# State-space scan in a two-block kernel: the block between the chunks computed once per group of four heads

## The chip, the cores and the metric

The kernel runs on one core of a Trainium2 chip. The metric is the device time of one execution in microseconds (us), as the median of several runs. Before the change it is 1258.52 us (three runs, 1258.48 to 1260.17). The core's engines work side by side and meet at semaphores: TensorE (PE; matmuls, with its weight loads shown apart as PEld), VectorE (DVE), ScalarE (ACT), GpSimd (POOL), and SyncE (SP), whose queue issues the weight DMAs.

## What is computed

The reference is two transformer-like blocks on 256 tokens of width 1024. Nearly all of the work is dense products with weights from HBM. The change touches one part of the second block, the state-space mixer (SSD): 32 heads of width 64 in 8 groups of four heads; the heads of a group share B and C. The 256 tokens are two chunks of 128.

```python
def step(state, inp):                      # one chunk of 128 tokens
    xc, dtc, bc, cc = inp
    cum = jnp.cumsum(dtc * A, axis=1)
    seg = cum[:, :, None] - cum[:, None, :]
    decay = jnp.exp(jnp.where(causal, seg, -jnp.inf))
    cb = jnp.einsum('btgn,bsgn->btsg', cc, bc)
    w = cb[..., None] * decay * dtc[:, None]
    y = jnp.einsum('btsgk,bsgkp->btgkp', w, xc)
    y = y + jnp.einsum('btgn,bgkpn->btgkp', cc, state) * jnp.exp(cum)[..., None]
    ...                                    # state for the next chunk
```

With two chunks and a zero first state, the output is a lower triangular 2 by 2 arrangement of 128x128 blocks per head: chunk 0 on chunk 0, chunk 1 on chunk 1 (both causal), and the block between the chunks, inputs of chunk 0 on outputs of chunk 1. A head's decay in that last block splits into a factor of the input token (decay to the end of chunk 0) and one of the output token (decay since the start of chunk 1).

## The kernel before

Weights come in "units" of up to 128x2048 float32 through a ring of five slots. ACT copies a unit to its rounded part `whi` (L830, in halves L841), DVE makes the rest `wlo` (L1310, in halves L1335), and PE does each product as three matmuls in the fast format (helper `three`, L2125 to L2127). Each engine's program is a fixed list of instructions, written out by hand and executed in order.

**The scan stage** is interleaved with the dense products of 16 units (`SSD_UNITS`): eight of the gate projection `zz`, then eight of the output projection `so`. Each unit has four steps; a step on PE is `ssd_step(n)` followed by six dense 512-column matmuls. `SSD_STEPS` says what each of the 64 steps carries. Steps 0 to 3 are empty, steps 4 to 15 are heads 0 to 11, steps 16 and 17 are empty; then head 12 (step 18), yT 0 (19), head 13 (20), yT 1 (21), heads 14 to 19 (22 to 27), two empty steps (28, 29), head 20 (30), yT 2 (31), head 21 (32), yT 3 (33), heads 22 to 27 (34 to 39), two empty (40, 41), head 28 (42), yT 4 (43), head 29 (44), yT 5 (45), heads 30 and 31 (46, 47), and the tail (48). ACT, DVE and PE each walk this list in their own order:

- SP broadcasts the head's decay row from DRAM to a ring of six buffers `dec` (L680), POOL adds a causal mask to the two diagonal blocks (L787).
- ACT, `decay(h)` (L1110): two exponentials over 256 and 128 columns, after POOL's mask. Between them it does the halves of `whi`, the tanh of the gates (L1123, in units 2, 4, 6, 8), the copies `xs_copy` (L854), the norm scaling (L1108) and the transposed output (L864).
- DVE, at head h: multiplies the 384 decay columns with the group's scores in PSUM bank `CB` (L1933). At h%8==6 it adds the y bank of the even group (L1879), at h%8==7 `prepare` makes the next eight heads' inputs (L1869 and L1873, four instructions of 512 columns), at h%8==2 it adds the odd group and gates (L1888), at h%8==3 `group_stats` (L1901). Further there are halves of `wlo` (two per four steps), the gate product (L1923) at the third step of units 2, 4, 6, 8, and at yT steps the low part (L1364).
- PE, at head h's step: `ssd_y_of(h - 2)`, three matmuls of 128x64 (L2729 to L2731), each in two passes. The step before a new group also computes that group's scores (`ssd_scores`, L2716 and L2717). At a yT step it transposes finished output (L2748).

So the product of head h is two head steps behind its place in the DVE list. Ahead of the stage, around line 1830 and 2688, the cumulative sums of all heads are made, negated, transposed and stored as rows of 384 columns.

Of the kernel before, what the change touches and what calls it, by code (L numbers as in the profile page):

```python
# [33 lines left out]
F32 = mybir.dt.float32  # L34
# [448 lines left out]
def build(nc, w, out):  # L483
# [3 lines left out]
    with ctx:  # L487
# [31 lines left out]
        crow = sb("crow", [SSD_HEADS, TRI])  # L519
        dec0 = sb("dec0", [P, TRI])  # L520
        decay_rows = nc.dram_tensor("decay_rows", (SSD_HEADS, TRI), F32, kind="Internal").ap()
# [55 lines left out]
        dec = [dec0[:, :]] + [rows[:, 1, TRI * b:TRI * b + TRI] for b in range(2)] + [room(14336 + TRI * b, TRI) for b in range(3)]  # L577
# [43 lines left out]
        dt_sum, dt_log, dta_ready, cum_row = sem("dt_sum"), sem("dt_log"), sem("dta_ready"), sem("cum_row")  # L621
# [45 lines left out]
        def _(sp):  # L667
# [46 lines left out]
        def _(pool):  # L714
# [66 lines left out]
            pool.wait_ge(cum_row, 1)  # L781
            pool.dma_start(decay_rows[:, :], crow[:, :]).then_inc(rows_stored, 16)
            for h in range(SSD_HEADS):
                pool.wait_ge(row_landed[h % SSD_RING], 16 * (h // SSD_RING + 1))
                d = dec[h % SSD_RING]
                diagonal = d.rearrange("p (a t) -> p a t", a=3)[:, 0:3:2, :]
# [26 lines left out]
        def _(act):  # L813
# [287 lines left out]
            nc.scalar.preload_act_table_set("exp_and_others")  # L1101

# [7 lines left out]
            def decay(h):  # L1110
                act.wait_ge(row_masked, h + 1)
                d = dec[h % SSD_RING]
                A(d[:, 0:T], d[:, 0:T], ACT.Exp, bias=negcum[:, 0, 0, h:h + 1])
                A(d[:, T:TRI], d[:, T:TRI], ACT.Exp, bias=negcum[:, 1, 0, h:h + 1]).then_inc(s_exp, 1)

            for u in range(SSD_UNITS):
                for n, (what, h) in enumerate(SSD_STEPS[SSD_PER_UNIT * u:SSD_PER_UNIT * (u + 1)]):
# [12 lines left out]
                    if what == "head":  # L1130
                        if h > 0:
                            decay(h)
# [158 lines left out]
        def _(dve):  # L1291
# [529 lines left out]
            for m in range(16):  # L1821
# [4 lines left out]
                if m == 5:  # L1826
# [3 lines left out]
                    V.tensor_scalar(negcum[:, :, :, :], sums.unsqueeze(2).to_broadcast([P, NT, 2, SSD_HEADS]), -1.0, None, ALU.mult)\  # L1830
                        .then_inc(done("cum"), 1)
                if m == 7:
                    b = wait_bank(dve, "cumT")
                    H = SSD_HEADS
                    mark(V.tensor_scalar(crow[:, 0:P], b[0:H, 0:P], -1.0, None, ALU.mult))
                    V.tensor_scalar(crow[:, 2 * P:TRI], b[0:H, P:2 * P], -1.0, None, ALU.mult).then_inc(done("cumT"), 1)
                    dve.wait_ge(dve_step, steps[0])
                    wait_drained(dve, "cumT")
                    V.tensor_scalar(crow[:, P:2 * P], crow[:, 2 * P:TRI], crow[:, P - 1:P], None, ALU.add).then_inc(cum_row, 1)
# [11 lines left out]
                if m == 0:  # L1851

                    dve.wait_ge(dt_log, 2)
# [5 lines left out]
            def prepare(q):  # L1859
# [11 lines left out]
                for t in range(NT):  # L1871
                    x3 = xsN[:, t, cols].rearrange("p (h d) -> p h d", d=SSD_P)
                    V.tensor_tensor(x3, x3, dtv[:, t, hs].unsqueeze(2).to_broadcast([P, 8, SSD_P]), ALU.mult).then_inc(xdt_ready, 1)  # L1873

# [33 lines left out]
            prepare(0)  # L1908
            last_norm = [what for what, _ in SSD_STEPS].index("tail") // SSD_PER_UNIT
            for u in range(SSD_UNITS):  # L1910
                for n, (what, h) in enumerate(SSD_STEPS[SSD_PER_UNIT * u:SSD_PER_UNIT * (u + 1)]):
# [13 lines left out]
                    if what == "head":  # L1925
# [3 lines left out]
                        if h > 8 and h % 8 == 3:  # L1929
# [179 lines left out]
        def _(pe):  # L2109
# [569 lines left out]
            for m, j in enumerate(BC_ORDER):  # L2679
                if m >= 2:  # L2680
                    b_unit(at[("bc", j)], h_hi, h_lo, one(("bc", j)), ready=(lambda k: second_block() if k == 3 else None) if m == 2 else None)
                if m == 4:

                    pe.wait_ge(dta_ready, 2)
                    pe.wait_ge(cst_in, 16)
                    b = claim("cum")
                    for t in range(NT):
                        last = M(b[:, SSD_HEADS * t:SSD_HEADS * (t + 1)], tri, dta[:, t, :], start=True, stop=True)
                    last.then_inc(fill("cum"), 1)
                if m == 7:  # L2690
                    wait_drained(pe, "cum")
                    b = claim("cumT")
                    for t in range(NT):
                        last = nc.tensor.transpose(b[0:2 * SSD_HEADS, P * t:P * t + P], negcum[:, t, :, :].rearrange("p a h -> p (a h)"), ident)
# [16 lines left out]
            y_bank, so_banks = [], []  # L2711

            def ssd_scores(g):
# [3 lines left out]
                M(b[:, T:TRI], bcT[:, g, P:T], bcT[:, 8 + g, P:T], start=True, stop=True).then_inc(fill(("CB", g)), 1)  # L2717

            def ssd_y_of(h):
# [5 lines left out]
                if h % 4 == 0:  # L2725
                    y_bank[:] = [claim(("y", h // 4))]
                y_0, y_1 = [y_bank[0][:, T * t + SSD_P * (h % 4):T * t + SSD_P * (h % 4) + SSD_P] for t in range(NT)]
                s = dec[h % SSD_RING]
                M(y_0, s[:, 0:P], xsN[:, 0, xs], start=True, stop=True)  # L2729
                M(y_1, s[:, P:T], xsN[:, 0, xs], start=True, stop=False)  # L2730
                M(y_1, s[:, T:TRI], xsN[:, 1, xs], start=False, stop=True).then_inc(ssd_y, 1)  # L2731

            def ssd_step(n):
                what, h = SSD_STEPS[n]
                if what == "head":
                    if h >= 2:
                        ssd_y_of(h - 2)
                if what == "tail":
# [246 lines left out]
```

## Time and profile before

| | |
|---|---|
| median of 3 runs | 1258.52 us |
| span of the profiled execution | 1257.2 us |
| PE busy | 1242.1 us (99%) |
| DVE busy | 932.5 us (74%) |
| ACT busy | 684.2 us (54%) |
| POOL busy | 68.2 us (5%) |
| DMA queue with the weights | 53.5% of 16 engines' span |
| scan stage | about 671 to 779 us |

The span is the profiled time from first to last instruction; the time of a run lies 1.3 us above it. "Busy" counts instructions, and a PE row's length includes its pipeline's drain, so the distance between two starts is what a matmul costs in a stream. A bracket behind a row is the engine's idle time before it, with what ended it.

### The profile page before, as it was taken

The numbers are of one execution on the slowest core, as the hardware profiler recorded it, in microseconds if no ns is written. First come the engines' busy times: TensorE is split into PE (matmuls) and PEld (weight loads), VectorE is DVE, ScalarE is ACT, GpSimd is POOL, SyncE is SP. The second block draws the span as 40 slices with busy tenths as digits, with TensorE's granted clock in tenths as the row PEclk, the third lists the DMA queues.
The fourth block names the chain that finished last, engine by engine and source line by source line (L and its number), as shares of the span: only waits on it lengthen the run. The fifth ranks groups of instructions, "written<-read, shape, count | busy, mean of one in ns | idle before, by whom it ended". The sixth has DMA issues, their size and how long they took to land. (4 is left out here: it accounts for less than half of the span.)

```text
span 1257.2 us, 18334 instructions
## 1 busy us (share of the span) xinstructions
PE 1242.1 (99%) x7514; PEld 1102.9 (88%) x7514; DVE 932.5 (74%) x1292; ACT 684.2 (54%) x872; POOL 68.2 (5%) x93
## 2 busy tenths in 40 slices
PE   9999999999999999999999999999999999999997
PEld 8878999989988888889998888888888888888886
DVE  6676857875456666577997998788888868788877
ACT  6654444343553444455777655466655574566652
POOL 2000000100000000000003331000000000000000
PEclk9999999999999999999999999999999999999999
DMA  9664545656435665647656654655554744655551
GB/s 294 219 184 144 185 143 188 214 186 209 168 101 170 199 194 178 197 138 219 185 168 210 203 191 151 217 185 201 184 186 138 231 134 134 201 194 179 197 194 41
DMA packets 162595, 227.97 MB, mean 181 GB/s; under 512 B 7853, under 2 KB 123825, under 8 KB 162384
## 3 DMA queue, kind: packets, MB, share of 16 engines
q1 hardware_dynamic: 159392, 216.68, 53.5%
q0 software_dynamic: 2816, 9.52, 2.3%
q8 instruction: 60, 0.98, 0.3%
q10 hardware_dynamic: 304, 0.59, 0.1%
q14 instruction: 23, 0.19, 0.0%
HBM read 225.68 MB, written 1.10 MB: 180 GB/s over the span
## 5 line engine op out<-in xcount | busy, mean ns | idle before, releaser
L1310 DVE TENSOR_TENSOR wlo<-raw,whi 128x2048 fp32r<-128x2048 f32 (+3 forms) x185 | 415.9, 2260 | 113.9 <-ACT whi L830 112.8
L830 ACT ACTIVATE whi<-raw 128x2048 fp32r<-128x2048 f32 (+3 forms) x185 | 345.9, 1883 | 16.0 <-DMA raw<-in_w_xkv 6.1
L2159 PE MATMUL psum<-h_both,whi 128*128 128x512 f32 x714 | 254.7, 396 | 0.0
L2158 PE MATMUL psum<-h_both,wlo 128*128 128x256 f32 x714 | 199.4, 279 | 0.3 <-DVE h_both L1364 0.3
L2125 PE MATMUL psum<-h_both,whi 128*128 128x256 f32 x688 | 195.9, 285 | 0.0
L2127 PE MATMUL psum<-h_both,wlo 128*128 128x256 f32 x688 | 194.6, 283 | 0.0
L2126 PE MATMUL psum<-h_both,whi 128*128 128x256 f32 x688 | 194.6, 283 | 0.0
L2125 PE MATMUL psum<-whi,r_hi 128*128 128x512 f32 x446 | 176.6, 396 | 0.0
L2127 PE MATMUL psum<-whi,r_lo 128*128 128x512 f32 x446 | 173.9, 390 | 0.0
L2126 PE MATMUL psum<-wlo,r_hi 128*128 128x512 f32 x446 | 173.8, 390 | 0.0
L2159 PEld LDWEIGHTS psum<-h_both,whi 128*128 128x128 f32 x714 | 134.0, 188 | 27.6
L2158 PEld LDWEIGHTS psum<-h_both,wlo 128*128 128x128 f32 x714 | 134.6, 189 | 5.2 <-DVE h_both L1364 0.6
L2125 PEld LDWEIGHTS psum<-h_both,whi 128*128 128x128 f32 x688 | 131.9, 192 | 0.4 <-issue 0.3
L2126 PEld LDWEIGHTS psum<-h_both,whi 128*128 128x128 f32 x688 | 131.9, 192 | 0.2
L2127 PEld LDWEIGHTS psum<-h_both,wlo 128*128 128x128 f32 x688 | 131.9, 192 | 0.0
L2125 PE MATMUL psum<-whi,h_both 128*128 128x512 f32 (+4 forms) x304 | 118.7, 391 | 0.4 <-issue 0.3
L1964 DVE SCALAR_TENSOR_TENSOR arena<-arena,pv 128x256 f32<-128x256 f32 x176 | 77.3, 482 | 51.7 <-ACT arena L1165 43.9
L2127 PE MATMUL psum<-whi,h_both 128*128 128x512 f32 (+4 forms) x304 | 113.5, 373 | 0.0
L2126 PE MATMUL psum<-wlo,h_both 128*128 128x512 f32 (+4 forms) x304 | 113.1, 372 | 0.0
L2127 PEld LDWEIGHTS psum<-whi,r_lo 128*128 128x128 f32 x446 | 83.7, 188 | 17.9
L2126 PEld LDWEIGHTS psum<-wlo,r_hi 128*128 128x128 f32 x446 | 83.9, 188 | 16.5
L2125 PEld LDWEIGHTS psum<-whi,r_hi 128*128 128x128 f32 x446 | 83.8, 188 | 15.3
(350 smaller groups left out, 1807.1 us busy)
## 6 DMA issues: line engine op xcount, KB each, us to landing
raw<-in_ffn_up SPq DMA_DIRECT2D x40, 1024.0 KB, 5.1
raw<-in_w_in SPq DMA_DIRECT2D x31, 1024.0 KB, 5.8
raw<-in_ssd_in_proj SPq DMA_DIRECT2D x22, 1024.0 KB, 5.4
raw<-in_ffn_down SPq DMA_DIRECT2D x22, 1024.0 KB, 4.9
raw<-in_w_up SPq DMA_DIRECT2D x16, 1024.0 KB, 5.6
raw<-in_w_down SPq DMA_DIRECT2D x16, 1024.0 KB, 4.9
raw<-in_w_xkv SPq DMA_DIRECT2D x8, 1024.0 KB, 5.2
raw<-in_ssd_out_proj SPq DMA_DIRECT2D x8, 1024.0 KB, 5.2
```

Source lines behind the costliest of these rows:

```text
L830: A(whi[u % SLOTS][:, 0:kt * n], raw[u % SLOTS][:, 0:kt * n], ACT.Copy).then_inc(hi_split, 1)
L1310: V.tensor_tensor(wlo[s][:, 0:kt * n], raw[s][:, 0:kt * n], whi[s][:, 0:kt * n].bitcast(F32), ALU.subtract).then_inc(lo_split, 1)
L1964: ins = V.scalar_tensor_tensor(y, fpad[g % 2][x][:, ct, tap:tap + T], pv[:, wcol:wcol + 1], y, ALU.mult, ALU.add)
L2125: M(o, a_hi, b_hi, start=start, stop=False)
L2126: M(o, a_hi, b_lo, start=False, stop=False)
L2127: return M(o, a_lo, b_hi, start=False, stop=stop_)
L2158: M(b[:, 0:T], w_lo_k, h_hi[:, k, :], start=False, stop=False)
L2159: return M(b[:, :], w_hi_k, h_both[:, :, k, :], start=False, stop=k == kt - 1)
```

## The change

The block between the chunks is no longer part of each head's matrix. `dec` has 256 columns per head, the two diagonal blocks; the decay rows are 256 long. Per group of four heads there is one product instead: PE takes the copied scores block `cbT` as stationary and the group's inputs scaled to the end of chunk 0 (`x_end`, 256 columns) as moving operand, DVE scales the result in PSUM in place, and the heads' own products accumulate on top. The order of the lists (`SSD_STEPS`) is the same.

```diff
+        after = dec0[:, 0:P]
+        x_end = [dec0[:, 0:T], room(14848, T)]
+        cbT = [room(15104 + P * b, P) for b in range(2)]
+        to_end, since = negcum[:, 0, 1, :], negcum[:, 1, 1, :]
...
-                elif h == 3:
+                elif h == 4:
                     wait_bank(sp, ("xsN", 7))
...
-            rows_at = {at[("zz", 0, 0)] + SLOTS - 1: [0, 1, 2], at[("zz", 0, 1)] + SLOTS: [3, 4, 5]}
+            rows_at = {at[("zz", 0, 0)] + SLOTS - 1: [0, 1, 2, 3], at[("zz", 0, 1)] + SLOTS: [4, 5]}
...
             nc.scalar.preload_act_table_set("exp_and_others")
+            wait_drained(act, "cum")
+            A(to_end, to_end, ACT.Exp).then_inc(factors_ready, 1)
+            A(since, negcum[:, 1, 0, :], ACT.Exp, scale=-1.0).then_inc(factors_ready, 1)
+
+            def copy_scores(g):
+                b = wait_bank(act, ("CB", g))
+                if g >= 2:
+                    act.wait_ge(off_done, g - 1)
+                A(cbT[g % 2], b[:, P:T], ACT.Copy).then_inc(cb_copied, 1)
...
-                A(d[:, 0:T], d[:, 0:T], ACT.Exp, bias=negcum[:, 0, 0, h:h + 1])
-                A(d[:, T:TRI], d[:, T:TRI], ACT.Exp, bias=negcum[:, 1, 0, h:h + 1]).then_inc(s_exp, 1)
+                A(d[:, 0:P], d[:, 0:P], ACT.Exp, bias=negcum[:, 0, 0, h:h + 1])
+                A(d[:, P:T], d[:, P:T], ACT.Exp, bias=negcum[:, 1, 0, h:h + 1]).then_inc(s_exp, 1)
...
                     if what == "head":
+                        if h % 4 == 0:
+                            copy_scores(h // 4)
                         if h > 0:
                             decay(h)
...
+            def scale_to_end(g):
+                dve.wait_ge(xdt_ready, 2 * (g // 2) + 2)
+                dve.wait_ge(factors_ready, 2)
...
+                V.tensor_tensor(x_end[g % 2].rearrange("p (h d) -> p h d", d=SSD_P),
+                                xsN[:, 0, 256 * g:256 * g + 256].rearrange("p (h d) -> p h d", d=SSD_P),
+                                to_end[:, heads].unsqueeze(2).to_broadcast([P, 4, SSD_P]), ALU.mult).then_inc(x_end_ready, 1)
+
+            def scale_off(g):
+                dve.wait_ge(off_done, g + 1)
+                y = bank[use[("y", g)][0]][:, T:2 * T].rearrange("p (h d) -> p h d", d=SSD_P)
+                V.tensor_tensor(y, y, since[:, 4 * g:4 * g + 4].unsqueeze(2).to_broadcast([P, 4, SSD_P]), ALU.mult).then_inc(off_scaled, 1)
...
             prepare(0)
+            scale_to_end(0)
...
                         b = wait_bank(dve, ("CB", h // 4))
-                        V.tensor_tensor(dec[h % SSD_RING], dec[h % SSD_RING], b[:, 0:TRI], ALU.mult)\
+                        if h % 4 == 0:
+                            dve.wait_ge(cb_copied, h // 4 + 1)
+                        d = dec[h % SSD_RING].rearrange("p (a t) -> p a t", a=2)
+                        V.tensor_tensor(d, d, b[:, 0:2 * T].rearrange("p (a t) -> p a t", a=2)[:, :, 0:P], ALU.mult)\
                             .then_inc(done(("CB", h // 4)) if h % 4 == 3 else s_w, 1)
+                        if h % 4 == 1:
+                            scale_off(h // 4)
                         if h % 8 == 6:
                             add_sums(2 * q)
                         if h % 8 == 7 and q < 3:
                             prepare(q + 1)
+                        if h % 4 == 3 and h < SSD_HEADS - 1:
+                            scale_to_end(h // 4 + 1)
...
+                    last = M(b[:, 2 * SSD_HEADS:3 * SSD_HEADS], after, dta[:, 0, :], start=True, stop=True)
...
+            def ssd_off(g):
+                pe.wait_ge(cb_copied, g + 1)
+                pe.wait_ge(x_end_ready, g + 1)
+                y_next[:] = [claim(("y", g))]
+                M(y_next[0][:, T:2 * T], cbT[g % 2], x_end[g % 2], start=True, stop=True).then_inc(off_done, 1)
...
                 if h % 4 == 0:
-                    y_bank[:] = [claim(("y", h // 4))]
+                    y_bank[:] = y_next
+                    pe.wait_ge(off_scaled, h // 4 + 1)
...
-                M(y_0, s[:, 0:P], xsN[:, 0, xs], start=True, stop=True)
-                M(y_1, s[:, P:T], xsN[:, 0, xs], start=True, stop=False)
-                M(y_1, s[:, T:TRI], xsN[:, 1, xs], start=False, stop=True).then_inc(ssd_y, 1)
+                M(y_0, s[:, 0:P], xsN[:, 0, xs], start=False, stop=True, skip_group_check=True)
+                M(y_1, s[:, P:T], xsN[:, 1, xs], start=False, stop=True, skip_group_check=True).then_inc(ssd_y, 1)
...
                     if h >= 2:
                         ssd_y_of(h - 2)
+                    if h % 4 == 0:
+                        ssd_off(h // 4)
```

Ahead of the stage, `crow` is made by one DVE instruction instead of three, the copy of `to_end` and the mask `after` are one small DVE instruction each, and the two transposes of the sums have 32 columns instead of 64.

## Rows read from the trace of the kernel before

**Rows 1.** The page: busy time by engine, and the granted clock in 40 slices

```profile
PE 1242.1 (99%) x7514; PEld 1102.9 (88%) x7514; DVE 932.5 (74%) x1292; ACT 684.2 (54%) x872; POOL 68.2 (5%) x93
...
PEclk9999999999999999999999999999999999999999
```

**Rows 2.** Waits of PE, 600 to 800 us: us in total, times, longest us

```profile
PE psum L2748 <- ACT arena L1108: 0.9, 3, 0.3
```

**Rows 3.** Timeline of PE, steps 34 to 36: start, length, engine, line, shapes

```profile
735.30 0.33 PE L2729 MATMUL psum<-arena,rows 128*128 128x64 f32 x2
735.47 0.39 PE L2730 MATMUL psum<-arena,rows 128*128 128x64 f32 x2
735.69 0.39 PE L2731 MATMUL psum<-arena,rows 128*128 128x64 f32 x2
735.89 0.48 PE L2125 MATMUL psum<-whi,r_hi 128*128 128x512 f32 x1
...
737.36 0.33 PE L2729 MATMUL psum<-arena 128*128 128x64 f32 x2
...
737.97 0.65 PE L2716 MATMUL psum<-arena 128*128 128x256 f32 x2
738.46 0.38 PE L2717 MATMUL psum<-arena 128*128 128x128 f32 x2
...
740.08 0.33 PE L2729 MATMUL psum<-arena 128*128 128x64 f32 x2
```

**Rows 4.** Timeline of PE, start of step 4, then head 1's product at step 7

```profile
673.37 0.47 PE L2125 MATMUL psum<-whi,h_both 128*128 128x512 f32 x1
...
678.94 0.43 PE L2729 MATMUL psum<-arena,rows 128*128 128x64 f32 x2 [0.30 <-DVE rows L1933]
```

**Rows 5.** Timeline of ACT at the start of the stage

```profile
672.19 1.28 ACT L1101 ACT_TABLE_LOAD   x1
673.48 1.06 ACT L841 ACTIVATE whi<-raw 128x1024 fp32r<-128x1024 f32 x1
674.45 0.49 ACT L1113 ACTIVATE dec<-dec,negcum 128x256 f32<-128x256 f32 x1
...
675.14 1.05 ACT L841 ACTIVATE whi<-raw 128x1024 fp32r<-128x1024 f32 x1
676.09 0.57 ACT L854 ACTIVATE arena<-psum 128x512 f32<-128x512 f32 x1
676.56 1.05 ACT L841 ACTIVATE whi<-raw 128x1024 fp32r<-128x1024 f32 x1
```

**Rows 6.** Timeline of PE, the product of head 2 at step 8

```profile
681.75 0.33 PE L2729 MATMUL psum<-arena,rows 128*128 128x64 f32 x2
```

**Rows 7.** Timeline of DVE, steps 33 to 36

```profile
735.05 0.88 DVE L1364 SCALAR_TENSOR_TENSOR r_lo<-psum,pv,r_hi 128x256 fp32r<-128x256 f32 x2 [1.32 <-ACT r_hi L864]
...
737.04 0.55 DVE L1933 TENSOR_TENSOR arena<-arena,psum 128x384 f32<-128x384 f32 x1
737.50 0.68 DVE L1879 TENSOR_TENSOR arena<-arena,psum 128x512 f32<-128x512 f32 x1
...
739.24 0.54 DVE L1933 TENSOR_TENSOR arena<-arena,psum 128x384 f32<-128x384 f32 x1
...
743.03 0.54 DVE L1933 TENSOR_TENSOR dec<-dec,psum 128x384 f32<-128x384 f32 x1
```

**Rows 8.** Timeline of PE, transposes of yT 1 and yT 3

```profile
708.75 0.60 PE L2748 MATMUL psum<-cst,arena 128*128 128x128 f32 x4
...
733.47 0.60 PE L2748 MATMUL psum<-cst,arena 128*128 128x128 f32 x4
```

**Rows 9.** Timeline of DVE around the other two `prepare`

```profile
685.11 0.56 DVE L1933 TENSOR_TENSOR arena<-arena,psum 128x384 f32<-128x384 f32 x1 [0.31 <-ACT arena L1114]
...
693.50 0.54 DVE L1933 TENSOR_TENSOR rows<-rows,psum 128x384 f32<-128x384 f32 x1
...
716.81 0.54 DVE L1933 TENSOR_TENSOR arena<-arena,psum 128x384 f32<-128x384 f32 x1
```

More of the change, by code:

```diff
@@ L518, in build @@
         expa = sb("expa", [P, SSD_HEADS])
-        crow = sb("crow", [SSD_HEADS, TRI])
+        crow = sb("crow", [SSD_HEADS, T])
         dec0 = sb("dec0", [P, TRI])
-        decay_rows = nc.dram_tensor("decay_rows", (SSD_HEADS, TRI), F32, kind="Internal").ap()
+        decay_rows = nc.dram_tensor("decay_rows", (SSD_HEADS, T), F32, kind="Internal").ap()
         ARENA = 15500
@@ L576, in build @@
         yN = [room(12288 + 1024 * b, NT, MIX) for b in range(2)]
-        dec = [dec0[:, :]] + [rows[:, 1, TRI * b:TRI * b + TRI] for b in range(2)] + [room(14336 + TRI * b, TRI) for b in range(3)]
+        dec = [rows[:, 1, T * b:T * b + T] for b in range(4)] + [room(14336 + T * b, T) for b in range(2)]
+        after = dec0[:, 0:P]
+        x_end = [dec0[:, 0:T], room(14848, T)]
+        cbT = [room(15104 + P * b, P) for b in range(2)]
+        to_end, since = negcum[:, 0, 1, :], negcum[:, 1, 1, :]
         knT, vmN, qnT = room(0, 8, T), room(2048, NT, D), room(4096, 8, T)
@@ L620, in build @@
         low_out = sem("low_out")
-        dt_sum, dt_log, dta_ready, cum_row = sem("dt_sum"), sem("dt_log"), sem("dta_ready"), sem("cum_row")
+        dt_sum, dt_log, dta_ready = sem("dt_sum"), sem("dt_log"), sem("dta_ready")
+        factors_ready, cb_copied, x_end_ready, off_done, off_scaled = (
+            sem(n) for n in ("factors_ready", "cb_copied", "x_end_ready", "off_done", "off_scaled"))
         s_conv, s_silu, xdt_ready, s_w, ssd_y, y_done = (sem(n) for n in ("s_conv", "s_silu", "xdt_ready", "s_w", "ssd_y", "y_done"))
@@ L1829, in _ @@
                     sums = b[:, 0:2 * SSD_HEADS].rearrange("p (t h) -> p t h", t=NT)
-                    V.tensor_scalar(negcum[:, :, :, :], sums.unsqueeze(2).to_broadcast([P, NT, 2, SSD_HEADS]), -1.0, None, ALU.mult)\
-                        .then_inc(done("cum"), 1)
+                    V.tensor_copy(to_end, b[:, 2 * SSD_HEADS:3 * SSD_HEADS])
+                    V.tensor_scalar(negcum[:, :, 0, :], sums, -1.0, None, ALU.mult).then_inc(done("cum"), 1)
                 if m == 7:
                     b = wait_bank(dve, "cumT")
[L1834 to L1839, printed above, removed]
+                    V.tensor_scalar(crow[:, :], b[0:SSD_HEADS, 0:T], -1.0, None, ALU.mult).then_inc(done("cumT"), 1)
                 wait_drained(dve, key)
@@ L1851, in _ @@
                 if m == 0:
+                    V.tensor_scalar(after, tri, -1.0, 1.0, ALU.mult, ALU.add).then_inc(dta_ready, 1)
                     dve.wait_ge(dt_log, 2)
@@ L1873, in prepare @@
                     V.tensor_tensor(x3, x3, dtv[:, t, hs].unsqueeze(2).to_broadcast([P, 8, SSD_P]), ALU.mult).then_inc(xdt_ready, 1)
+            def scale_to_end(g):
+                dve.wait_ge(xdt_ready, 2 * (g // 2) + 2)
+                dve.wait_ge(factors_ready, 2)
+                if g == 1:
+                    wait_bank(dve, ("xsN", 7))
+                if g >= 2:
+                    dve.wait_ge(off_done, g - 1)
+                heads = slice(4 * g, 4 * g + 4)
+                V.tensor_tensor(x_end[g % 2].rearrange("p (h d) -> p h d", d=SSD_P),
[5 more added lines that the diff above has]
+                V.tensor_tensor(y, y, since[:, 4 * g:4 * g + 4].unsqueeze(2).to_broadcast([P, 4, SSD_P]), ALU.mult).then_inc(off_scaled, 1)
             def add_sums(g):
@@ L2682, in _ @@
                 if m == 4:
-                    pe.wait_ge(dta_ready, 2)
+                    pe.wait_ge(dta_ready, 3)
                     pe.wait_ge(cst_in, 16)
@@ L2687, in _ @@
                     for t in range(NT):
-                        last = M(b[:, SSD_HEADS * t:SSD_HEADS * (t + 1)], tri, dta[:, t, :], start=True, stop=True)
+                        M(b[:, SSD_HEADS * t:SSD_HEADS * (t + 1)], tri, dta[:, t, :], start=True, stop=True)
+                    last = M(b[:, 2 * SSD_HEADS:3 * SSD_HEADS], after, dta[:, 0, :], start=True, stop=True)
                     last.then_inc(fill("cum"), 1)
@@ L2693, in _ @@
                     for t in range(NT):
-                        last = nc.tensor.transpose(b[0:2 * SSD_HEADS, P * t:P * t + P], negcum[:, t, :, :].rearrange("p a h -> p (a h)"), ident)
+                        last = nc.tensor.transpose(b[0:SSD_HEADS, P * t:P * t + P], negcum[:, t, 0, :], ident)
                     last.then_inc(fill("cumT"), 1)
@@ L2708, in _ @@
             xs_transpose(6)
-            y_bank, so_banks = [], []
+            y_bank, y_next, so_banks = [], [], []
             def ssd_scores(g):
```

4 lines of the change are left out of this document (2 added, 2 removed).

## The prediction

> **What bounds the kernel now.** I read the page first [rows 1]: PE is busy for 1242.1 of 1257.2 us, and every slice shows the granted clock at 9, the higher of its two levels, 2.4 GHz. So the kernel ends when PE's list ends, and a change counts by what it does to that list: the work in it, and the gaps at its waits. Work saved on DVE or ACT is worth nothing unless PE waits for it. Second, the waits of PE around the scan stage [rows 2]: 0.9 us at three of the transposes, whose input comes from ACT. Third, the timelines of PE, ACT and DVE in the stage, side by side. They say how far each engine is from PE's next need, and that decides here, because the change adds waits to PE.
>
> **PE's work.** The three matmuls of a head start at 735.30, 735.47 and 735.69, the dense product after them at 735.89 [rows 3]. A middle one takes 0.22 us, and the whole block 0.59. Taking one out of each of 32 heads saves 32 x 0.22 = 7.0 us (6.3 at the mean of 0.20). The Trainium skill has a rule that would price this otherwise ("TensorE: Matmul & The Clock Gate", section "Back-to-back issue gap"): start to start is the column count over 2.4 GHz plus 2.5 ns, so two passes of 64 columns cost 0.06 us and the 32 removed ones 1.8 us. The rows show 0.11 us per pass, which is that page's time for a weight load of 128 columns (section "LDWEIGHTS"); with such a load before each pass, the measured 0.22 us is the price to take.
>
> Added are eight products of 128x256. The nearest row has the same shape: the scores' first product starts at 737.97 and its successor at 738.46 [rows 3], so 0.49 us, eight times 3.9 us. The product at step 4 stands alone between dense ones; after such a block the first dense matmul is late by some 0.1 us. The third column block in `cum` ahead of the stage is at most one small matmul, 0.2 us. Sum: -7.0 + 3.9 + 0.1 + 0.2 = **-2.8 us**, between -2.0 and -3.2.
>
> For the waits I need the length of PE's steps. A step with a head takes 2.06 us now (735.30 to 737.36), and the step with scores 2.72 us (737.36 to 740.08) [rows 3]. An empty step is 2.06 - 0.59 - 0.08 = 1.39 us. After the change a head's block takes 0.37 to 0.39, so its step takes 1.84 us, with scores 2.5.
>
> **The wait at step 4.** `ssd_off(0)` waits for `copy_scores(0)`. PE begins step 4 at 673.37 [rows 4]. In ACT's list the copy comes after the table load, half a unit, `decay(0)`, the other half and `xs_copy(7)`; ACT gets there at 676.56 [rows 5]. Added before it are the two exponentials of 128x32. No row of the stage has that size; two exponentials over 384 columns take 0.69 us (674.45 to 675.14), so a small one takes between 0.1 and 0.3, and I take 0.3 for both, with 0.2 and 0.6 as ends. `decay(0)` is 0.1 shorter. The copy of 128 columns ends 0.3 to 0.4 after its start (the 512-column one takes 0.57). It is done at 676.56 + 0.3 - 0.1 + 0.35 = 677.1, so PE stands still for **3.8 us** (3.6 to 4.1). Queued behind PE's waiting instruction are all dense products. `decay(1)` and the half units sit behind the copy on ACT, later by 0.5 us only, which the pause of PE covers. What goes in return: from step 4 to head 2's product at step 8 PE takes 8.38 us (673.37 to 681.75) [rows 4, 6], where the steps' work is 1.37 + 1.45 + 2.06 + 2.71 = 7.6. So 0.8 us of waiting for ACT and DVE is there already, the 0.30 at 678.94 among it [rows 4], and the new pause swallows it.
>
> **The wait at the even groups.** `ssd_off(g)` also waits for `x_end`. In DVE's list `scale_to_end(g)` stands behind head 4g-1; where g is even it thereby stands behind the whole `prepare` too. Before, the first thing PE needed from behind `prepare` was head 4g's matrix, two head steps later. Now it needs it at head 4g's own step.
>
> DVE doesn't run ahead of PE there, since it is tied to it shortly before: at yT steps its L1364 waits for ACT's copy of PE's transpose (idle 1.32 us) [rows 7]. So the times can be counted from PE's transpose, whatever was delayed earlier.
> - New DVE prices: 384 columns last 0.55 us and 512 columns 0.68 [rows 7], that is 0.13 per 128 columns. `dec` times scores becomes 0.13 shorter. `scale_to_end` and `scale_off`, 256 columns, last 0.42; overlapped with their neighbours they add 0.33 each (384 columns add 0.46, from 737.04 to 737.50).
> - Group 6: PE's yT 3 is at 733.47 [rows 8], DVE is through `prepare` at 743.03 [rows 7], 9.56 later. Two shorter products and the new scaling make it 9.56 - 0.26 + 0.33 = 9.6. PE arrives after 1.81 (transposes, six dense ones) + 1.84 + 2.5 + 0.39 = 6.5. Pause: **3.1 us**.
> - Group 4: yT 1 at 708.75 [rows 8], `prepare` over at 716.81 [rows 9], so 8.06, then 8.1 against 6.5: **1.6 us**. It is shorter because no gate product (L1923) falls between.
> - Group 2: here DVE hangs on ACT, whose tanh needs the banks full at PE's step 8; head 5 waits 0.31 for it at 685.11, and `prepare` is over at 693.50 [rows 9], 11.75 after PE's step 8 at 681.75 [rows 6]. With `scale_off(1)`, `scale_to_end(2)`, three shorter products and a shorter `decay`: 11.9. PE arrives after 2.3 + 1.84 + 1.84 + 2.5 + 0.39 = 8.9. Pause: **3.0 us**, or 2.3 if this `prepare` is as quick as the next.
>
> Between them each estimate can be off by 0.5 us.
>
> **Waits that stay covered.** At odd groups there is no `prepare` before the scaling and, from group 3, two empty steps; the margin is smallest at group 5, which has a gate product in between. `off_scaled` is needed at head 4g+2's step and stands behind head 4g+1 on DVE. After a pause PE takes 0.49 + 1.45 + 1.84 = 3.8 us to get there, DVE 0.33 + 1.14 + 0.33 + 0.33 = 2.1 (a half unit is the 1.14, from 737.50 + 0.60 to 739.24 [rows 7]). At group 1 there is no pause before: DVE's head 5 is 3.36 us after PE's step 8 (685.11 less 681.75) [rows 6, 9], the scaled result 0.33 - 0.1 + 0.33 later, at 3.9; PE gets there after 2.3 + 1.84 = 4.1, a margin of 0.2 us. Claiming the y bank two steps earlier waits for nothing: the bank's last sum is in DVE's list before the `x_end` that PE waits for anyway. ACT's copies of groups 1 to 7 have a dense block of 1.4 us to hide in, and ACT is waiting at that time. The three waits for the transposes, 0.9 us [rows 2], go away, since DVE starts its chain to them from the end of PE's pause. POOL's masks and SP's decay rows keep their places, and the rows are shorter; both follow PE's pace, as SP's weights do.
>
> **Sum.** 3.8 + 3.0 + 1.6 + 3.1 = 11.5 us of pauses, -0.8 and -0.9 for waits that they replace, -2.8 of work: +7.0. Span 1257.2 + 7.0 = 1264.2. The run's time stands 1.3 us above the span, so **1265.5 us**. Nothing behind the stage gives it back: PE has no gap there that these pauses could fill. With the low and high end of each term the sum runs from +4 to +9.5: 1262.5 to 1268.
>
> **Rivals.**
> - *The clock falls.* No row of before shows PE below the higher level, but none shows a pause of 3 us either. The Trainium skill (same page, section "HAM oscillation — how this bites in real kernels") says that a long pause between bursts of matmuls sends the clock back to the low level until PE has been busy again. At half the clock a step's six dense matmuls take 1.4 us more. Two or three such steps behind one pause: 2.8 to 4.2 us, about 1269 us. The pauses at step 4 and group 6 are the candidates. For it: their length. Against: they are single pauses in dense work. 12%.
> - *Only the pause at step 4 is real*, because DVE is earlier at the even groups than I count. It would have to gain 3 us on PE between the transpose and `prepare`, but its list there is full. Then +3.8 - 1.7 - 2.8 = -0.7: 1257.8 us, no difference. 9%.
> - *All is hidden* and PE's lighter list decides: -2.8 - 1.7 gives 1254 us. The point from which this holds is an ACT that reaches the copy by 673.4 as well, and it is 3 us late by its own rows [rows 5]. 4%.
> - *The scaled result is late too.* If the margins of 0.2 and 0.7 us at groups 1 and 5 are gone, 1 to 2 us are added: 1267 us. 5%, inside the range.
> - The forecast: 70%.
>
> **Range and chances.** 1260.5 to 1269.5 us takes in the forecast's own range, the late scaling and half of the clock's case, and leaves out the two hidden cases. A measurement of this kernel tells 0.2% (2.5 us) from no change. Faster by more: 5%; within: 10%; slower by more: 85%.
>
> **What would show it.** In the waits of PE after: one of 3.5 to 4 us released by ACT at step 4, and three released by DVE's scaling before the products of groups 2, 4 and 6, of 3.0, 1.6 and 3.1 us. PE's busy time lower by 3 us. The clock at 9 in all slices, else the first rival holds. No wait left at the transposes. If the pause at group 6 is under 1.5 us, DVE was less tied to PE than its rows say, and the middle of the sum is wrong. If a head's block falls by less than 0.15 us, the price of the removed matmul was wrong.

## The result and the profile after

The changed kernel takes 1274.0 us (median of 4 runs, 1273.33 to 1275.31) against 1259.35 us for the kernel before in the same comparison: ratio 1.0119, 95% interval 1.0107 to 1.0131. It is slower, as forecast, but by 14.7 us, where 7.0 was forecast and the range ended at 1269.5 us.

The page of the changed kernel, the lines that answer to [rows 1]:

```profile
span 1271.5 us, 18290 instructions
...
PE 1245.3 (98%) x7468; PEld 1104.9 (87%) x7468; DVE 933.4 (73%) x1308; ACT 682.4 (54%) x882; POOL 69.1 (5%) x93
...
PEclk9999999999999999999999899999999999999999
```

PE has 46 instructions fewer and is busy 3.2 us longer, and one slice of the clock shows 8. PE's waits between 600 and 800 us, the answer to [rows 2] (total, times, longest):

```profile
PE psum L2765 <- issue: 8.7, 3, 3.2
PE psum L2765 <- ACT arena L1116: 3.8, 1, 3.8
```

L2765 is the shared product. The wait for ACT's copy is the one at step 4; the other three, which the view puts down to "issue", end when DVE's scaling to the chunk's end is done. The waits at the transposes are gone. PE's timeline at the four places where it paused (start, length, bracket: idle time before):

```profile
677.41 0.67 PE L2765 MATMUL psum<-dec,arena 128*128 128x256 f32 x2 [3.83 <-ACT arena L1116]
677.73 0.58 PE L2165 MATMUL psum<-whi,h_both 128*128 128x512 f32 x1
678.15 0.40 PE L2166 MATMUL psum<-wlo,h_both 128*128 128x512 f32 x1
678.38 0.40 PE L2167 MATMUL psum<-whi,h_both 128*128 128x512 f32 x1
...
679.35 0.63 PE L2167 MATMUL psum<-whi,h_both 128*128 128x512 f32 x1
679.78 0.63 PE L2165 MATMUL psum<-whi,h_both 128*128 128x512 f32 x1
...
698.55 0.67 PE L2765 MATMUL psum<-dec,arena 128*128 128x256 f32 x2 [2.99 <-issue]
...
726.06 0.72 PE L2765 MATMUL psum<-dec,arena 128*128 128x256 f32 x2 [2.53 <-issue]
...
754.26 1.19 PE L2765 MATMUL psum<-dec,arena 128*128 128x256 f32 x2 [3.18 <-issue]
```

The pauses are 3.83, 2.99, 2.53 and 3.18 us. Behind the first one, dense matmuls start 0.23 us apart at 678.15 and 0.43 apart at 679.35: PE has gone to half its clock. The same in a table by stretch (PE, PEld, DVE, ACT, POOL busy, then the granted clock, DMA share, GB/s):

```profile
668.00:700.00 32.00, 25.17 (x121) 21.05 (x120) 24.06 (x38) 20.41 (x45) 9.03 (x10) 0.93 0.51 166
700.00:730.00 30.00, 27.47 (x133) 23.25 (x133) 24.40 (x46) 17.27 (x37) 8.96 (x10) 0.90 0.47 142
730.00:766.00 36.00, 32.82 (x165) 27.73 (x165) 29.54 (x60) 15.94 (x37) 10.87 (x11) 0.95 0.46 139
```

Before, the clock is 1.00 in all of them. Microsecond by microsecond behind the first pause it reads:

```profile
678.00:679.00 1.00, 1.00 (x6) 0.75 (x5) 1.00 (x2) 1.00 (x4) 0.19 (x1) 0.88 0.36 125
679.00:680.00 1.00, 1.00 (x4) 0.81 (x3) 1.00 (x4) 1.00 (x3) 1.00 (x2) 0.50 0.00 0
680.00:681.00 1.00, 1.00 (x3) 0.77 (x3) 1.00 (x1) 0.97 (x3) 0.29 (x1) 0.50 0.00 0
681.00:682.00 1.00, 1.00 (x4) 0.74 (x3) 1.00 (x3) 0.00 (x0) 0.00 (x0) 0.50 0.00 0
682.00:683.00 1.00, 1.00 (x8) 0.92 (x7) 0.04 (x1) 0.00 (x0) 0.00 (x0) 0.92 0.00 0
```

The shares of the clock that are missing in these five rows (0.12, 0.5, 0.5, 0.5 and 0.08 us) make 1.7 us. That is what one low stretch costs if PE works all through it. Over 671 to 801 us the mean clock is 0.95, so all four cost about 130 x 0.05 = 6.5 us.

The account of the span: +12.5 us of pauses, +6.5 of low clock, -1.7 for waits that are gone, -2.8 for PE's lighter list: +14.5. Measured: 1271.5 - 1257.2 = 14.3. The pauses and the clock are read from this trace; -1.7 and -2.8 are the forecast's own terms. PE's busy time bears the last one out: it grew by 3.2 us although 6.5 us of low clock are in it, so the work itself is some 3.3 us less.

### The profile page after: what moved, and what is told of

It reads as the page before. It is cut to its first block, busy times and chain, and to the rows that moved or that the text cites. A ratio compares the mean times of both kernels' runs of the same rounds, so it can differ in the third digit from the quotient of the medians.

```text
span 1271.5 us, 18290 instructions
## 1 busy us (share of the span) xinstructions
PE 1245.3 (98%) x7468; PEld 1104.9 (87%) x7468; DVE 933.4 (73%) x1308; ACT 682.4 (54%) x882; POOL 69.1 (5%) x93
## 4 chain that ended last, share of the span: by engine, by line
PE 90%; DVE 5%; issue 2%; ACT 2%; DMA 1%; SPq 0%; DVEq 0%
PE psum L2165 20%; PE psum L2167 20%; PE psum L2166 20%; PE psum L2199 13%; PE psum L2198 7%; PE psum L2196 2%; PE psum L2197 1%; DVE xn L1498 1%; DVE xn L1488 1%; DVE psum L1474 1%; DVE bn L1475 1%; PE psum L2779 1%; PE psum L2545 1%; PE psum L2524 1%; DMA raw<-in_w_in 1%
## 5 line engine op out<-in xcount | busy, mean ns | idle before, releaser
L2165 PE MATMUL psum<-whi,h_both 128*128 128x512 f32 (+4 forms) x304 | 120.9, 398 | 0.8 <-issue 0.7
L2167 PE MATMUL psum<-whi,h_both 128*128 128x512 f32 (+4 forms) x304 | 115.1, 378 | 0.0
```

The source lines that it names most:

```text
L2165: M(o, a_hi, b_hi, start=start, stop=False)
L2167: return M(o, a_lo, b_hi, start=False, stop=stop_)
```

## The experiments

Medians stand beside the kernel before in the same comparison, whose median lay between 1258.77 and 1258.94 us.

One thing outside the stage blurs differences of 1 to 2 us. Near 980 us PE waits twice for a norm on DVE. Here are these waits (total, times, longest) and the 15 us around them, first in the kernel before and then in a8_stats_first, a variant described below:

```profile
PE psum L2239 <- DVE xn L1481: 1.5, 2, 0.9
975.00:990.00 15.00, 13.44 (x82) 12.51 (x81) 12.90 (x22) 6.48 (x8) 2.22 (x4) 1.00 0.79 206
```

```profile
PE psum L2242 <- DVE xn L1481: 1.5, 2, 0.9
975.00:990.00 15.00, 13.44 (x72) 12.67 (x71) 11.51 (x20) 6.17 (x8) 2.13 (x4) 0.89 0.73 199
```

The waits are the same, but only the second execution has a low stretch behind them, worth 15 x 0.11 = 1.7 us. The traces of a4, a7 and f1 have it too, and each of these is one of its kernel's longer executions; those of a1, f2 and f3 don't, and are among the shorter ones. So a median can move by up to 1.6 us with how many of its executions have this stretch.

**Theory A:** each long pause of PE brings a low stretch, and these are what the forecast's sum lacked. **Rival B:** the low clock comes from the narrow products or from DVE's added work. Two kernels take pauses away.

```diff
 a2_no_rescale
-                        if h % 4 == 3 and h < SSD_HEADS - 1:
-                            scale_to_end(h // 4 + 1)
+                        if h == 3:
+                            scale_to_end(1)
...
-                pe.wait_ge(x_end_ready, g + 1)
+                pe.wait_ge(x_end_ready, min(g, 1) + 1)
```

> The changed kernel with the scaling to the chunk's end made for groups 0 and 1 only; the later groups' shared products use these two again, so nothing stands behind prepare for PE (the shared block's numbers are those of other groups). Theory A (each long pause of PE is followed by a stretch at the low clock, which costs 1.6 us more): the pauses of 3.0, 2.5 and 3.2 us go with three low stretches, 13.4 us below the changed kernel: 1260.6 us, one low stretch left, near step 4. Rival B (the low clock comes from the narrow products or from the added DVE work, not from the pauses): four low stretches stay, 8.7 us below: 1265.3 us.

1263.69 us, ratio 1.0034 (1.0022 to 1.0046). The three pauses are gone, and so are three of the four low stretches; in the stage the clock is below 1.00 only from 678 to 682 us. The narrow products are all still there, so they don't lower it; of DVE's added work a part is left out here, and a5_off_later below settles that half of B. But the time is 3 us above what A alone gives. PE's waits show most of it:

```profile
PE psum L2765 <- ACT arena L1116: 3.8, 1, 3.8
PE psum L2778 <- DVE psum L1905: 2.7, 3, 1.1
```

L1905 is `scale_off`. With the pauses at the even groups out of the way, the scaled result is late for heads 8, 16 and 24: the forecast's fourth rival, which the pauses had hidden. The profiled execution took 1262.2 us; the median, 1.5 us higher, belongs to executions with a lower mean clock (0.995 or 0.996 where it has 0.997).

```diff
 a3_copy_first
-        cbT = [room(15104 + P * b, P) for b in range(2)]
+        cbT = [dec0[:, T:TRI], room(15232, P)]
...
+            copy_scores(0)
             for u in range(SSD_UNITS):
...
-                        if h % 4 == 0:
+                        if h > 0 and h % 4 == 0:
                             copy_scores(h // 4)
```

> The changed kernel with ACT's copy of group 0's scores moved from behind xs_copy(7) to right behind the two small exponentials (its buffer moved to a free place). PE's pause at step 4 should shrink from 3.8 to 0.8 us. Theory A: with its low stretch gone, 4.6 us below the changed kernel, up to 0.8 us of it back as the old waits at heads 0 and 1: 1269.4 to 1270.2 us. Rival B (the low clock is not due to the pause): 3.0 us below or less: 1271 us or more, and the granted clock near 679 us still low.

1272.73 us, ratio 1.0107 (1.0091 to 1.0122). A miss by 3 us. The copy is early, but now PE waits 1.58 us for DVE's `x_end` at step 4 and 1.41 us for the scaled result at head 0. The pause was split rather than removed, so 0.8 us of it and one low stretch of 1.7 us are gone. That gives 1271.5 us, which two of the four executions show (1271.2 and 1271.9 us, mean clock 0.995). The other two (1273.6 and 1274.4 us, 0.992), of which the profiled one is the first, have more low clock: the low stretch with the pause of group 6 is twice as long, and one comes near 996 us, behind the waits for the norm.

```profile
748.00:760.00 12.00, 8.90 (x36) 7.35 (x35) 9.34 (x16) 4.07 (x9) 1.68 (x3) 0.72 0.39 118
990.00:1002.00 12.00, 10.09 (x51) 9.32 (x50) 9.47 (x15) 3.25 (x5) 1.64 (x3) 0.86 0.63 170
```

What A says holds: behind the two short pauses no row shows a lowered clock before 694 us.

a4_both has both of these edits.

> Both edits: copy first, and no rescaling behind prepare (the later groups' shared products use group 0's and 1's inputs). No pause above 1 us is left. Theory A: no low stretch; the changed kernel less 13.4 and 4.2: 1256.4 us, below the kernel before, ratio 0.998; up to 1.3 us more if the waits at the transposes return. Rival B: low stretches remain: 1262 us or more.

1260.4 us, ratio 1.0010 (1.0001 to 1.0020). No pause is above 1.5 us and the clock is 1.00 throughout the stage, as A has it. The missing 4 us are again DVE's:

```profile
PE psum L2779 <- DVE psum L1906: 4.3, 4, 1.4
PE psum L2766 <- DVE dec L1898: 1.3, 1, 1.3
```

**The step moved, the work kept.** 

```diff
 a5_off_later (PE)
-                    if h % 4 == 0:
+                    if h % 4 == 1:
                         ssd_off(h // 4)
```

> The changed kernel with the shared product of each group issued one head step later on PE (at head 4g+1 instead of 4g). PE comes 1.5 to 1.9 us later to each wait: pauses of about 2.3, 1.1, 0.7 and 1.3 us instead of 3.8, 3.0, 2.5 and 3.2, together 7.1 us less. Theory A (the low stretch needs a long pause): at most one low stretch is left, 4.8 us less again: 1262 us. If even the short pauses are followed by a low stretch: 1267 us. If the scaled result is then late for head 4g, 1 to 2 us come on top at each group.

1263.92 us, ratio 1.0042 (1.0027 to 1.0058). One move by one step takes away 10 of the 14.7 us, with all of the change's work kept. The pauses are 2.40, 1.17, 0.58 and 1.22 us, and only the first has a low stretch (granted clock in the last but two column):

```profile
677.00:682.00 5.00, 4.82 (x16) 4.03 (x17) 4.60 (x8) 3.78 (x9) 1.52 (x2) 0.66 0.24 85
696.00:701.00 5.00, 3.89 (x18) 3.07 (x19) 4.88 (x9) 1.01 (x3) 0.73 (x1) 1.00 0.61 224
```

The narrow products and DVE's added work are all there, and three low stretches are gone with the long pauses. So B is out.

**Pauses by themselves**, in the kernel before, in a part that the change doesn't touch:

```diff
 c1_pauses
             for what, g in MLP_ORDER[2:-2]:
+                if (what, g) in PAUSES:
+                    pe.wait_ge(idled, sum(PAUSE_OPS[:PAUSES.index((what, g)) + 1]))
...
+            for i, (what, g) in enumerate(PAUSES):
+                pool.wait_ge(unit_used, at[("down", g - 2)] + 1)
+                for j in range(PAUSE_OPS[i]):
+                    ins = nc.gpsimd.tensor_tensor(idle2[:, :, :], big2, big2, ALU.add).then_inc(idled, 1)
+                    pool.wait_ge(idled, sum(PAUSE_OPS[:i]) + j + 1)
```

> The kernel before with eleven pauses of PE in the first block's MLP, far from the scan: at the start of units up 3 to up 13 PE waits for 1, 2, 3, 4, 5, 1, 2, 3, 4, 5 and 3 instructions of POOL, each about 0.8 us, started when PE's last unit is done. The pauses should be about 1, 1.8, 2.6, 3.4, 4.2 us and so on, 28 us in all. Theory A: behind the pauses of 2.5 us and more the granted clock falls for some 3 us (cost 1.6 us each, six or seven times, 10 us), behind the short ones it stays: 1298 us. If a low stretch follows only some of them, the pause's place counts too. If it never falls here, a pause alone isn't enough, and the cause in the scan stage is something else: 1288 us.

1339.2 us (one run). The pauses came out longer than planned, 2.1 to 6.9 us and 56.4 in all, since POOL's first instruction of each pause lasted 1.9 to 2.3 us and the second 2.5, where only the further ones took 0.6. The total is 80.4 us over the kernel before, so 24 us more than the pauses. Three places of 8 us, with pauses of 2.44, 5.45 and 2.14 us:

```profile
418.00:426.00 8.00, 5.56 (x24) 4.60 (x23) 4.78 (x2) 1.63 (x1) 2.29 (x1) 0.79 0.43 136
454.00:462.00 8.00, 5.55 (x18) 4.74 (x19) 1.24 (x1) 0.00 (x0) 2.32 (x2) 0.57 0.21 74
511.00:519.00 8.00, 5.86 (x34) 5.10 (x34) 4.27 (x2) 1.12 (x1) 1.94 (x1) 1.00 0.44 131
```

The clock fell with the first two and stayed at 1.00 with the third. So a pause alone is enough, with neither narrow products nor DVE's work in play. Ten of eleven pauses, all but that of 2.14 us, have low clock with them. From each pause's end on it adds up to 46 us, in which PE works at half its speed: 23 of the 24 us, or some 2.3 us for each of the ten. The planned short pauses weren't reached here; the other kernels supply them.

**Why group 4's pause was longer than forecast.** 

```diff
 a6_no_masks
-                nc.gpsimd.tensor_tensor(diagonal, diagonal, big2, ALU.add).then_inc(row_masked, 1)
+                nc.gpsimd.tensor_tensor(d[:, 0:1], d[:, 0:1], big2[:, 0, 0:1], ALU.add).then_inc(row_masked, 1)
...
-                A(d[:, 0:P], d[:, 0:P], ACT.Exp, bias=negcum[:, 0, 0, h:h + 1])
+                A(d[:, 0:P], d[:, 0:P], ACT.Exp, scale=0.0)
```

> The changed kernel with POOL's mask cut to one column, and the exponentials taken of zero (the decays are then all one). It asks why prepare took 4.35, 3.94 and 3.6 us at groups 2, 4 and 6 where its four instructions take 2.6 us at the start of the stage. Theory: POOL's masks of 128x256 run beside it and slow DVE; then prepare takes 2.6 us everywhere, the pauses shrink to about 1.3, 1.2 and 2.2 us, and the time falls by 4 us and by up to three low stretches of 1.6 us: 1265 to 1270 us. Rival (the slow instructions are slow by themselves or through ACT): no change of prepare, 1274 us.

1264.35 us (one run). `prepare` of group 2, first in the changed kernel, then without the masks (DVE's timeline):

```profile
693.68 2.05 DVE L1882 TENSOR_TENSOR arena<-arena,row_d 128x512 f32<-128x512 f32 x2
695.76 2.23 DVE L1886 TENSOR_TENSOR arena<-arena,dtv 128x512 f32<-128x512 f32 x2
698.03 0.42 DVE L1897 TENSOR_TENSOR dec<-arena,negcum 128x256 f32<-128x256 f32 x1
```

```profile
692.77 1.29 DVE L1882 TENSOR_TENSOR arena<-arena,row_d 128x512 f32<-128x512 f32 x2
694.10 1.29 DVE L1886 TENSOR_TENSOR arena<-arena,dtv 128x512 f32<-128x512 f32 x2
695.43 0.42 DVE L1897 TENSOR_TENSOR dec<-arena,negcum 128x256 f32<-128x256 f32 x1
```

4.35 us become 2.66, so POOL's masks beside it cost DVE up to 1.7 us. The product with PSUM (L1969) lasts 0.41 us in both kernels: of the two kinds, those with two inputs from SBUF are slowed. ACT isn't the cause, although a6_no_masks changes its exponentials too: at the start of the changed kernel's stage `prepare` has ACT busy beside it, but no mask, and its instructions take 0.69 us each. This agrees with the Trainium skill, "SBUF — State Buffer", section "SBUF: two separate sides", which has DVE instructions with two SBUF inputs compete with POOL for a shared port.

**What PE's lighter list is worth.** The forecast counted -2.8 us in full.

```diff
 a1_no_between
-                M(y_1, s[:, P:T], xsN[:, 0, xs], start=True, stop=False)
-                M(y_1, s[:, T:TRI], xsN[:, 1, xs], start=False, stop=True).then_inc(ssd_y, 1)
+                M(y_1, s[:, T:TRI], xsN[:, 1, xs], start=True, stop=True).then_inc(ssd_y, 1)
```

> The kernel before with the middle matmul of each head left out (32 products of 128x64; the block between the chunks is then missing from the output). It measures PE's removed work by itself. Forecast's price, 0.22 us each: 7.0 us below the kernel before, ratio 0.9944. Rival, a pass priced by its columns alone (0.06 us each): 1.8 us below, ratio 0.9985. A third possibility: part of it comes back as longer waits for DVE at heads 0 and 1 and at the transposes, then 5 to 6 us.

1256.9 us, ratio 0.9984 (0.9975 to 0.9994): only 2.0 us. By the time alone the rival price (1.8 us) would seem to fit, but the profile says otherwise: the span is 2.4 us shorter, PE is busy 5.9 us less, and its waits are longer than in [rows 2]:

```profile
PE psum L2747 <- ACT arena L1108: 4.0, 3, 1.8
PE psum L2729 <- DVE rows L1933: 1.1, 2, 0.6
```

The waits for ACT grew by 3.1 us and those for DVE by 0.8, and 2.4 + 3.9 = 6.3 us, or 0.20 for each matmul. So the price of a removed matmul was about right (0.22, with 0.20 as its mean), but what came late next was the chain to the transposes: sums, gate, statistics (DVE), root (POOL), scaling (ACT). **Theory C:** this chain sets the pace as soon as PE is quicker. **Rival D:** DVE is full everywhere, so moving one piece only makes another late. The test takes a half unit of 1.2 us out of the chain:

```diff
 a7_lighter_stats_first (on a1), a8_stats_first (on before), f2_mended (on f1)
+                    behind = what == "head" and h > 8 and h % 8 == 3
-                    if n == 3 and u < last_norm:
+                    if n == 3 and u < last_norm and not behind:
                         lo_half(0)
...
                             .then_inc(done(("CB", h // 4)) if h % 4 == 3 else s_w, 1)
+                        if behind:
+                            lo_half(0)
```

> As a1_no_between (the middle matmul of each head left out, so the block between the chunks is missing), and DVE's half unit of 1.2 us at heads 11, 19 and 27 moved from ahead of group_stats to behind the head's product. In a1_no_between only 2.0 of 7.0 us arrived, and PE waited 0.97, 1.77 and 1.28 us at the transposes of yT 0, 2 and 4. Theory C (the chain sums, gate, statistics on DVE, root on POOL, scaling on ACT sets the pace of the stage, not PE's list): the chain is 1.14 us shorter, so these waits fall to 0, 0.6 and 0.15 us: 3.2 us less than a1_no_between, 1253.7 us, ratio 0.9960. Rival D (the waits are only the visible part of a DVE that is full everywhere): DVE is late at another place instead, 1256 to 1257 us.

1254.17 us, ratio 0.9965 (0.9953 to 0.9977): 2.7 us less than a1_no_between. PE's waits for ACT at the transposes are 1.0 us instead of 4.0. C holds; D has a small part, since one wait of 0.8 us for DVE is new.

> The kernel before with only the move of the half unit behind group_stats, nothing left out. Its waits at the transposes cost some 0.4 us each over three places. Theory C: they vanish, 1.0 to 1.3 us less, ratio 0.9991. Rival D: no difference.

1257.96 us, ratio 0.9991 (0.9982 to 1.0000). The waits at the transposes are gone from the profile. The interval touches 1, so the gain of about 1 us is likely rather than certain.

**Mended versions.** f1_mended keeps all the work of the change:

```diff
 f1_mended (besides copy_scores(0) as in a3 and ssd_off as in a5)
-                    if n == 1 and 0 < u < last_norm:
+                    if n == 1 and 0 < u < last_norm and not late(what, h):
                         lo_half(1)
...
                         if h % 8 == 7 and q < 3:
-                            prepare(q + 1)
+                            prepare(q + 1, (0,))
                         if h % 4 == 3 and h < SSD_HEADS - 1:
                             scale_to_end(h // 4 + 1)
+                        if h > 0 and h % 8 == 0:
+                            prepare(q, (1,))
...
-                        if h % 4 == 1:
+                        if h % 4 == 1 and h > 1 or h == 0:
                             scale_off(h // 4)
+                        if n == 1 and 0 < u < last_norm and late(what, h):
+                            lo_half(1)
```

Here `late` is true at head 8q+1 from q = 1 on.

> The changed kernel mended: ACT copies group 0's scores right behind the small exponentials; PE's shared product comes at head 4g+1; DVE makes the first token tile of prepare and then the scaling to the chunk's end, the second tile after the next head's product, and the half unit at the step of head 8q+1 after the scaled result. No work is left out. By the rows: PE reaches the shared product of groups 4 and 6 about 8.4 us after its transpose, DVE has the scaled inputs after 6.7 and 7.9, so no pause there. Theory A: no low stretch, PE's lighter list counts: 2.5 to 4 us below the kernel before, 1256 us, ratio 0.9975. Rival (DVE is full, and each moved piece makes something else late): small waits of 0.5 to 1.5 us at heads 8, 16, 24 and at the transposes, 1259 to 1263 us.

1259.76 us, ratio 1.0005 (0.9996 to 1.0013): in the stage no pause is above 1.33 us and no low stretch is left. It is 14 us better than the change, and no different from the kernel before. The rival was right. What is left:

```profile
PE psum L2807 <- ACT arena L1123: 2.6, 3, 1.3
PE psum L2787 <- DVE psum L1906: 0.8, 2, 0.5
```

> f1_mended with the half unit moved behind group_stats. f1_mended waited 0.85, 1.33 and 0.38 us at the transposes. Theory C: 2.4 us less than f1_mended, 1257.4 us, ratio 0.9987 to the kernel before. Rival D (DVE is full): the scaled results or heads' products are late instead, 1259 us, ratio 1.000.

1258.02 us, ratio 0.9990 (0.9981 to 0.9999): 1.7 us less. As C says, the wait of 2.6 us falls, to 0.2. The medians understate it. By time and mean clock only three of f2's eleven executions are of the shorter kind, without the low stretch near 980 us (1256.3 to 1256.8 us, clock 0.999; the others 1257.9 to 1258.6 us, 0.997 or 0.998). The five shortest of f1 lie at 1258.6 to 1259.1 us. Shorter against shorter, the move is worth 2.2 us.

```diff
 f3_pool (on f2: DVE's scaling to the chunk's end, from the second group on, goes to POOL)
-                        if h % 4 == 3 and h < SSD_HEADS - 1:
-                            scale_to_end(h // 4 + 1)
...
             for h in range(SSD_HEADS):
+                if h % 4 == 1 and h > 1:
+                    g = h // 4
+                    pool.wait_ge(xdt_ready, 2 * (g // 2) + 1)
...
+                    pool.wait_ge(off_done, max(g - 1, 1))
+                    nc.gpsimd.tensor_tensor(x_end[g % 2].rearrange("p (h d) -> p h d", d=SSD_P),
...
```

> f2_mended with the scaling to the chunk's end of groups 1 to 7 made by POOL, ahead of its mask for head 4g+1, instead of DVE. DVE's list is 7 x 0.33 = 2.3 us shorter. If DVE's fullness is what is left: 0.5 to 1.5 us less than f2_mended, 1256.5 us. Rival: POOL's instruction runs beside DVE's and slows it as the masks do, or POOL delays the masks and with them ACT's decays: 0 to 2 us more than f2_mended.

1255.83 us, ratio 0.9976 (0.9966 to 0.9986). This beats both kernels: 3.1 us below the kernel before, 18 below the change. PE's waits:

```profile
PE psum L2798 <- DVE psum L1916: 1.0, 2, 0.5
PE psum L2818 <- ACT arena L1133: 0.2, 1, 0.2
PE psum L2299 <- DVE xn L1509: 0.2, 1, 0.2
```

The median is 2.2 us below f2's, but that isn't the worth of DVE's lighter list: eight of f3's nine executions are of the shorter kind (1255.6 to 1256.5 us) where f2 has three in eleven. Shorter against shorter it is about 1 us, and the spans of the two profiled executions, neither with a low stretch near 980 us, differ by 1.3 (1254.9 and 1253.6). That is within the 0.5 to 1.5 us that were expected. Whether the edit itself makes the low stretch rarer isn't shown. POOL's instruction takes 0.6 to 0.8 us where DVE's takes 0.42.

## Why the prediction was wrong

The direction was right, and so was the cause of each pause, but the size wasn't: PE's clock behind the pauses, which the sum left out, and one pause that was put too short make up 7.4 us, and the measured time lies 7.3 us above the sum. By its steps:

- *The wait at step 4:* forecast 3.8 us, measured 3.83, released by ACT's copy. Right.
- *Group 6:* forecast 3.1, measured 3.18. Right. Counting from PE's transpose, to which DVE is tied, was a sound way to see how late DVE would be.
- *Group 2:* forecast 3.0, measured 2.99, but that close by luck. Two errors cancel: `prepare` started 7.1 us after PE's step 8, where it was 8.1 before, and it lasted 4.35 us, where it was 3.62. The rows are `prepare` before at groups 2 and 4, then PE's step 8 in the changed kernel, with `prepare` and the scaling of group 4:

```profile
689.88 1.90 DVE L1869 TENSOR_TENSOR arena<-arena,row_d 128x512 f32<-128x512 f32 x2
713.78 1.36 DVE L1869 TENSOR_TENSOR arena<-arena,row_d 128x512 f32<-128x512 f32 x2
```

```profile
686.59 0.33 PE L2778 MATMUL psum<-arena,rows 128*128 128x64 f32 x2
...
721.59 2.04 DVE L1882 TENSOR_TENSOR arena<-arena,row_d 128x512 f32<-128x512 f32 x2
723.67 1.83 DVE L1886 TENSOR_TENSOR arena<-arena,dtv 128x512 f32<-128x512 f32 x2
725.53 0.42 DVE L1897 TENSOR_TENSOR dec<-arena,negcum 128x256 f32<-128x256 f32 x1
```
- *Group 4:* forecast 1.6, measured 2.53. `prepare` took 3.94 us (721.59 to 725.53), where the forecast took over 3.03 from the kernel before (713.78 to 716.81 [rows 9]); a6_no_masks shows that its length depends on how many of POOL's masks fall beside it. The four rows of `prepare` before lay between 2.6 and 3.6 us, so this spread was to be seen and belonged in the term.
- *The clock:* this is the step that failed. It stood among the rivals with 12% and "two or three such steps behind one pause" at two candidate places. All four pauses came with a low stretch, even the shortest of 2.53 us; each cost about 1.6 us, together 6.5. So that rival had the effect but not its shape: about half of its price for a pause, at twice as many pauses. The sum put the term at nothing. The argument against it, single pauses in dense work, had no row behind it. a2, a4, a5 and c1 show that in the stage and in the first block the low stretches come and go with the long pauses.
- *Waits that they replace:* right, those at the transposes are gone.
- *PE's lighter list:* the work is nearly as priced (a1_no_between: 6.3 us for 7.0), and -2.8 us fits the account, but only because the pauses gave the next chain time. The lower price cited from the Trainium skill ("TensorE: Matmul & The Clock Gate", section "Back-to-back issue gap") was misread: that section gives the formula for an isolated matmul and says itself that it counts too little at small widths, where the weight load comes in. The trace agrees, with 0.20 us for a matmul. The rival "all is hidden" promised 1254 us by counting it in full. a4_both and f1_mended are that case, at 1260.4 and 1259.8 us: DVE's chain is late next. That rival's price was wrong by 6 us.
- *The scaled result:* forecast as covered in the changed kernel, and so it was. It came out as soon as the pauses shrank (a2, a3, a4). The margin of 0.7 us that the forecast gives for group 5 has no working behind it.

Left open: how much of f3_pool's gain over f2_mended comes from which place; what besides a pause's length decides whether the clock falls (below); and whether -0.8 us, the forecast's price for the waits that the first pause swallows, is exact.

## What to carry to other kernels

Where an engine is 99% busy, a change that takes work off it and adds waits to it is judged by the waits: find for each one what stands ahead of the releasing instruction in its engine's list, and whether that engine is tied to the waiting one shortly before. Add to a TensorE pause of 2.5 us or more the low clock that comes with it, here 1.6 us, about half of the pause again. Look at single executions before trusting a difference of 1 to 2 us between medians: one low stretch more or less is 1.6 us. And before counting lighter work as gain, look at the next chain with under 1 us of slack: in this stage it took 3.9 of 6.3 us.

## What the runs showed of the hardware

- With single pauses of 2.40, 2.44, 2.53, 2.99, 3.18 and 3.83 us in otherwise dense matmuls, with five of 2.52 to 3.76 us in a2_no_rescale, a3_copy_first and a6_no_masks, and with the nine of 4.8 to 6.9 us in c1_pauses, the granted clock fell from its higher level (2.4 GHz) to the lower (1.2 GHz). It didn't with 0.58, 1.17, 1.58 and 2.14 us, nor with one of 2.42 us in a6_no_masks:

```profile
746.00:752.00 6.00, 5.56 (x29) 4.77 (x30) 5.46 (x10) 0.97 (x2) 0.19 (x1) 1.00 0.53 189
```

  So near 2.4 us it went either way. The Trainium skill ("TensorE: Matmul & The Clock Gate", section "Why this matters for your kernels") puts the gap to avoid somewhat higher than the shortest pauses with a fall here; the measurements decide.
- It can fall without any such pause: behind two waits of 0.9 us and less, 1.5 us together, it did in a8_stats_first and did not in the kernel before. So a pause's length isn't all that counts.
- The fall needn't come in the pause: behind the one of 3.83 us PE ran 1.3 us at the higher level first.
- Longer pauses cost more than 1.6 us each (2.3 on average in c1_pauses).
- A DVE instruction with two SBUF inputs of 512 columns lasts 0.69 us alone and up to 1.23 beside POOL's masks; one with an input from PSUM isn't slowed (0.41 us in L1969, with a mask beside it or without).
